# Norm sums held as rows, modulation columns 32 wide, and the first head's levels as two 64-wide blocks

## The reference

```python
sh1, sc1, gt1, sh2, sc2, gt2 = jnp.split(mod, 6, axis=-1)        # mod = silu(c) @ w_mod + b_mod
h = rmsnorm(x, lw['g_mix']) * (1.0 + sc1) + sh1
pq, pkv, pkr, hq, hf_f, hf_b, hi, hg, ga, gb = split_cols(h @ lw['w_in'])
q = (rmsnorm(pq, lw['g_q']) @ lw['w_uq'])                        # ...
ckv = rmsnorm(pkv, lw['g_kv'])                                    # ...
# four heads of a gated linear recurrence, forward and backward over the tokens:
o = rmsnorm(o_f + o_b, g_hg.reshape(HG_HEADS, HG_DV))
o = o.reshape(B, T, HG_WIDTH).astype(hq.dtype) * jax.nn.silu(hg)
```

## Time and profile before

| | us |
| --- | --- |
| median of 3 runs | 2058.93 |
| the runs' ends | 2056.06 to 2059.39 |
| the profiled execution's own time | 2058.16 |
| its span, first to last instruction | 2056.4 |
| busy: PE | 1994.0 |
| busy: DVE | 1120.0 |
| busy: ACT | 766.7 |
| busy: POOL | 831.9 |

### The profile page before, as it was taken

The page is one execution under the profiler, slowest core; times in us unless marked ns, Lnnn a source line. Parts: engine busy times, 40 slices in busy tenths (PEclk is TensorE's granted clock), DMA queues, the critical chain, the costliest instruction groups (busy, mean ns, idle before and its releaser), DMA issues.

```text
span 2056.4 us, 34056 instructions
## 1 busy us (share of the span) xinstructions
PE 1994.0 (97%) x13708; PEld 1837.9 (89%) x13708; DVE 1120.0 (54%) x1715; ACT 766.7 (37%) x1189; POOL 831.9 (40%) x595
## 2 busy tenths in 40 slices
PE   6999999999999989999999988999999999999998
PEld 5888999999999978887799877999999999988886
DVE  5314353526142047566535356988888888645363
ACT  4323233333223254767733234322222222353441
POOL 1225263535133235455535634433443443252441
PEclk9999999999999999999999999999999999999999
DMA  8563111112213284324266445422222231584661
GB/s 294 200 199 37 42 51 44 48 52 74 67 41 90 72 227 143 93 67 107 73 173 202 147 149 189 125 77 65 86 65 65 75 98 59 175 304 141 230 237 67
DMA packets 223310, 244.09 MB, mean 119 GB/s; under 512 B 57865, under 2 KB 184162, under 8 KB 223154
## 3 DMA queue, kind: packets, MB, share of 16 engines
q1 hardware_dynamic: 220962, 233.65, 37.3%
q0 software_dynamic: 2192, 8.26, 1.2%
HBM read 182.62 MB, written 59.26 MB: 118 GB/s over the span
## 4 chain that ended last, share of the span: by engine, by line
PE 53%; DVE 3%; DMA 3%; ACT 2%; POOL 1%; issue 1%; SPq 1%; DVEq 0%; ACTq 0%; POOLq 0%
PE late_psum L2938 22%; PE late_psum L2950 13%; PE late_psum L1876 4%; PE late_psum L1901 4%; PE late_psum L2897 3%; PE late_psum L2251 3%; PE late_psum L1511 1%; PE late_psum L1846 1%; DMA s_w_raw<-in_w_hg_o 1%; DVE p_lo L2056 1%; DMA scratch_extra<-e_lo 1%; DMA merge_gates<-scratch_gates 0%; DVE conv L3124 0%; ACT prob L1987 0%; PE late_psum L1515 0%
## 5 line engine op out<-in xcount | busy, mean ns | idle before, releaser
L688 PE MATMUL s_psum<-h_hi,s_w_hi 128*128 128x384 f32 x984 | 333.3, 344 | 6.4 <-DVE h_lo L1402 6.4
L688 PE MATMUL s_psum<-h_hi,s_w_lo 128*128 128x384 f32 x984 | 326.1, 337 | 0.0
L688 PE MATMUL s_psum<-h_lo,s_w_hi 128*128 128x384 f32 x984 | 325.9, 337 | 0.0
L131 POOL TENSOR_TENSOR s_w_lo<-s_w_raw,s_w_hi 128x1024 fp32r<-128x1024 f32 x41 | 100.0, 2440 | 337.0 <-ACT s_w_hi L126 337.0
L2938 PE MATMUL late_psum<-h_lo,ffn_w_hi 128*128 128x320 f32 (+1 forms) x704 | 208.5, 296 | 0.0
L2938 PE MATMUL late_psum<-h_hi,ffn_w_lo 128*128 128x320 f32 (+1 forms) x704 | 208.4, 296 | 0.0
L2938 PE MATMUL late_psum<-h_hi,ffn_w_hi 128*128 128x320 f32 (+1 forms) x704 | 208.3, 296 | 0.0
L688 PEld LDWEIGHTS s_psum<-h_hi,s_w_hi 128*128 128x128 f32 x984 | 185.5, 189 | 15.8 <-issue 14.0
L688 PEld LDWEIGHTS s_psum<-h_lo,s_w_hi 128*128 128x128 f32 x984 | 186.1, 190 | 0.0
L688 PEld LDWEIGHTS s_psum<-h_hi,s_w_lo 128*128 128x128 f32 x984 | 185.8, 189 | 0.0
L2873 POOL TENSOR_TENSOR u_lo<-u_raw,u_hi 128x384 fp32r<-128x384 f32 x66 | 112.9, 1719 | 162.5 <-ACT u_hi L2770 161.5
(11 more groups left out here) (371 smaller groups left out, 4709.9 us busy)
## 6 DMA issues: line engine op xcount, KB each, us to landing
w_raw<-in_w_ffn_out SPq DMA_DIRECT2D x66, 512.0 KB, 3.7
ffn_raw<-in_w_ffn_in SPq DMA_DIRECT2D x44, 512.0 KB, 5.3
s_w_raw<-in_w_in SPq DMA_DIRECT2D x41, 512.0 KB, 4.3
s_w_mod<-in_w_mod SPq DMA_DIRECT2D x8, 2048.0 KB, 8.3
scratch_u<-conv SPq DMA_DIRECT2D x22, 576.0 KB, 3.6
u_raw<-scratch_u SPq DMA_DIRECT2D x66, 192.0 KB, 5.2
scratch_gates<-sig SPq DMA_DIRECT2D x48, 192.0 KB, 1.9
merge_gates<-scratch_gates SPq DMA_DIRECT2D x16, 576.0 KB, 4.8
```

What stands on the lines that cost most here:

```text
L131: pool.tensor_tensor(flat[0], flat[1], flat[2], ALU.subtract).then_inc(self.lo_ready, 1)
L688: return pe.matmul(slot_bank(s), weights(c)[wx][:, k, :], hx[:, k, j * CH:(j + 1) * CH], start=(k == 0 and n == 0), stop=(k == KD - 1 and ...
```

## The change

- The norms' and heads' sums: three matmuls with 32 columns of ones as stationary (`ones[:, 0:BLOCK]`) and 384 tokens moving, chunk g into partitions 32g to 32g + 31 of one bank. The statistic is now 96x384 and lies in rows; root and reciprocal run on it, in place. The broadcast is three matmuls, one for each chunk, with a row of ones as stationary and the statistic's row moving.
- The columns of `m_rows` and `mod_rows` (`piece_columns`, `mod_columns`): 16 matmuls of 32x2 in place of 4 of 128x2, at 12 places.
- The first head's levels 1 to 6 (h == 0): two 64-wide blocks a tile in place of four of 32.
- The table: R, kv_rb, q_rb, q_apply, up_load and up_split one slot later. ACT's S waits for the R of the head before (`rb_ps`), since the statistic is in place. The heads' statistic lies on the memory of `mod_rows`.
- ACT's start: split(0) and split(1) move ahead of the last `x_take` and of `take_piece(0)`.

Lines number from the kernel before and after: after, the product is L692, the levels L829, S L898, R L906, the columns L781.

```diff
+ROWS = slice(0, NCH * BLOCK)
...
         self.acc = arena(f"{tag}_acc", [P, NT])
-        self.stat = arena(f"{tag}_stat", [P, 2 * TILES])
+        self.stat = arena(f"{tag}_stat", [P, CH])
...
         pe.wait_ge(self.acc_ready, self.kts - 1)
-        for t in range(TILES):
-            last = pe.matmul(psum[:, t:t + 1], self.acc[:, t * P:(t + 1) * P], self.cst.ones[:, 0:1], start=True, stop=True)
+        for g in range(NCH):
+            last = pe.matmul(psum[BLOCK * g:BLOCK * (g + 1), 0:CH], self.cst.ones[:, 0:BLOCK], self.acc[:, g * CH:(g + 1) * CH],
+                             start=True, stop=True)
...
         act.wait_ge(self.sums_ready, 1)
-        act.activation(self.stat[:, 0:TILES], psum[:, 0:TILES], ACT.Sqrt, scale=1.0 / self.width,
-                       bias=self.cst.eps[:, 0:1]).then_inc(self.std_ready, 1)
+        act.activation(self.stat[ROWS, :], psum[ROWS, 0:CH], ACT.Sqrt, scale=1.0 / self.width,
+                       bias=self.cst.eps[ROWS, 0:1]).then_inc(self.std_ready, 1)
...
         dve.wait_ge(self.std_ready, 1)
-        dve.reciprocal(self.stat[:, TILES:2 * TILES], self.stat[:, 0:TILES]).then_inc(self.rstd_ready, 1)
+        dve.reciprocal(self.stat[ROWS, :], self.stat[ROWS, :]).then_inc(self.rstd_ready, 1)
...
         pe.wait_ge(self.rstd_ready, 1)
-        for t in range(TILES):
-            last = pe.matmul(psum3[:, t // 3, (t % 3) * P:(t % 3 + 1) * P],
-                             self.stat[:, TILES + t:TILES + t + 1].to_broadcast([P, P]), self.cst.ident[:, :],
-                             start=True, stop=True)
+        for g in range(NCH):
+            row = slice(BLOCK * g, BLOCK * g + 1)
+            last = pe.matmul(psum3[:, g, 0:CH], self.cst.ones[row, :], self.stat[row, :], start=True, stop=True)
...
             at[a + 1 + lv].append(("L", h, lv))
-        for r, kind in ((9, "X"), (10, "U"), (12, "O"), (13, "S"), (14, "R")):
+        for r, kind in ((9, "X"), (10, "U"), (12, "O"), (13, "S"), (15, "R")):
...
             at[a - HG_PHASE + 15].append(("Q", h, 0))
-    for r, kind in ((6, "kv_square"), (7, "kv_sums"), (8, "kv_rb"), (9, "cache"), (10, "kv_apply"), (11, "key"),
-                    (13, "ckv_out"), (18, "q_square"), (20, "q_sums"), (21, "q_rb"), (22, "q_apply"), (26, "up_load"), (30, "up_split")):
+    for r, kind in ((6, "kv_square"), (7, "kv_sums"), (9, "kv_rb"), (9, "cache"), (10, "kv_apply"), (11, "key"),
+                    (13, "ckv_out"), (18, "q_square"), (20, "q_sums"), (22, "q_rb"), (23, "q_apply"), (27, "up_load"), (31, "up_split")):
...
         near = early("hg_near", [P, TILES, SIDE])
+        rows_at = early.at
...
         sel = early("mod_sel", [P, 8])
-        ostat = early("ostat", [P, 2 * TILES])
+        orow = Arena(nc, rows_at)("ostat", [P, CH])
...
                             a = 4 * x + 2 * j
-                            last = pe.matmul(psum[:, 7, a:a + 2], m_rows[i % 2][:, x, j * P:(j + 1) * P], sel[:, 0:2],
-                                             start=True, stop=True)
+                            for b in range(0, P, BLOCK):
+                                last = pe.matmul(psum[b:b + BLOCK, 7, a:a + 2], m_rows[i % 2][:, x, j * P + b:j * P + b + BLOCK],
+                                                 sel[:, 0:2], start=True, stop=True)
...
                         a = 8 * n + 2 * j
-                        last = pe.matmul(psum[:, 5, a:a + 2], mod_rows[n % 2][:, j * P:(j + 1) * P], sel[:, 0:2],
-                                         start=True, stop=True)
+                        for b in range(0, P, BLOCK):
+                            last = pe.matmul(psum[b:b + BLOCK, 5, a:a + 2], mod_rows[n % 2][:, j * P + b:j * P + b + BLOCK],
+                                             sel[:, 0:2], start=True, stop=True)
...
                                 t = 3 * g + x
+                                if h == 0 and 0 < lv < LEVELS:
+                                    b = 1 << (lv - 1)
+                                    for i in range(2):
+                                        dst = psum[i * SIDE:(i + 1) * SIDE, level_bank(n), x * SIDE:(x + 1) * SIDE]
+                                        own = t * P + i * SIDE
+                                        last = pe.matmul(dst.rearrange("p (n h b) -> p n h b", h=2, b=b),
+                                                         k_level[lv % 2][:, own:own + SIDE], sibling_view(qd, own, SIDE, b),
+                                                         start=True, stop=True)
+                                    continue
...
                         pe.wait_ge(osq_ready, 3 * h + 3)
-                        for t in range(TILES):
-                            last = pe.matmul(psum[:, S_BANK, t:t + 1], osq[:, t * P:(t + 1) * P], cst.ones[:, 0:1],
-                                             start=True, stop=True)
+                        for g in range(NCH):
+                            last = pe.matmul(psum[BLOCK * g:BLOCK * (g + 1), S_BANK, 0:CH], cst.ones[:, 0:BLOCK],
+                                             osq[:, g * CH:(g + 1) * CH], start=True, stop=True)
...
                         pe.wait_ge(gated_ready, 3 * h + 3)
-                        for t in range(TILES):
-                            last = pe.matmul(psum[:, rb_bank(t // 3), (t % 3) * P:(t % 3 + 1) * P],
-                                             ostat[:, TILES + t:TILES + t + 1].to_broadcast([P, P]), cst.ident[:, :],
-                                             start=True, stop=True)
+                        for g in range(NCH):
+                            row = slice(BLOCK * g, BLOCK * g + 1)
+                            last = pe.matmul(psum[:, rb_bank(g), 0:CH], cst.ones[row, :], orow[row, :], start=True, stop=True)
...
                         act.wait_ge(s_ps, h + 1)
-                        act.activation(ostat[:, 0:TILES], psum[:, S_BANK, 0:TILES], ACT.Sqrt, scale=1.0 / DK,
-                                       bias=cst.eps[:, 0:1]).then_inc(std_ready, 1)
+                        if h > 0:
+                            act.wait_ge(rb_ps, h)
+                        act.activation(orow[ROWS, :], psum[ROWS, S_BANK, 0:CH], ACT.Sqrt, scale=1.0 / DK,
+                                       bias=cst.eps[ROWS, 0:1]).then_inc(std_ready, 1)
...
                         x_take(2 * t - 3)
+                split(0)
+                split(1)
...
                 take_piece(0)
-                split(0)
-                split(1)
...
                         dve.wait_ge(std_ready, h + 1)
-                        dve.reciprocal(ostat[:, TILES:2 * TILES], ostat[:, 0:TILES]).then_inc(rstd_ready, 1)
+                        dve.reciprocal(orow[ROWS, :], orow[ROWS, :]).then_inc(rstd_ready, 1)
```

## The result

The changed kernel takes 2026.14 us (median of 4 runs, 2022.51 to 2027.25) against 2059.16 before (median of 4, 2056.06 to 2059.58): a ratio of 0.9843, 95% interval 0.9830 to 0.9857. That is 33 us off where 24.4 were forecast. The profiled execution of after is 2027.25 us long, against 2058.16: 30.9 off. It is the slowest of the four runs of after, 1.1 above their median.

The account below looks back on a forecast made before the run. TensorE, busy 97% of the span, was taken to bound the kernel; −3.8 − 2.5 − 6.0 − 6.2 − 6.2 + 2.3 − 3.0 + 1.0 = −24.4 against 2058.16 gave 2034 us, range 2025 to 2045.

Parts of the forecast that it names:

- start, POOL beside DVE: Before TensorE's first product: ACT's earlier splits let POOL's subtractions finish before DVE's gain_mix; −3.8 us.
- clock behind it: 8 us behind the start gap, clock at 0.50 of full: most of the lost work returns; −2.5 us.
- columns, 12 sites: Modulation columns: 32 records of 32x2 matmuls at 12 ns each replace a 0.88 us step; −6.0 us.
- S and R, 6 sites each: Norm sums and broadcast in four heads, kv, q: each 1.93 us falls to 0.9; −6.2 us apiece.
- levels 64 wide: First head's levels 1 to 6: 18 64-wide multiplications replace 36 32-wide, a loss of +2.3 us.
- stall: First head, 164.60 to 172.50: instructions late behind SP's `mod` stores; a third of 9.3 us goes, −3.0 us.
- q's new wait: Chunk after q_apply: POOL's qn_lo starts later, w_lo ends later, TensorE waits; +1.0 us.
- behind the first stage: After about 716 us: all that the change touches lies in the first stage, so no term was summed here.
- The rival in which a record needs 25 ns: Column steps: 32 records need 0.8 us, the 12 sites give only −1.0; 2038.8 us, chance 0.03.
- Row groups side by side: R's three one-row matmuls at partitions 0, 32, 64 overlap, 0.9 us; if in turn, 2.2, chance 0.22.
- the rival with stall and low clock gone: First head and start: stores no longer meet TensorE's packet, low clock vanishes; 6.3 and 1.5 more off, 2026, chance 0.13.
- The moved steps: R, kv broadcast, up_load and up_split one slot later: no cost; q_apply's move priced separately at +1.0 us.

Follow-up runs that it names:

- the kernel before with late stores: Kernel before the change, only SP's four row stores of `mod` moved from the first head's fourth slot to its thirteenth: 2047.93 us, ratio 0.9950.
- The kernel with 32-wide levels: Changed kernel with the first head's levels 1 to 6 as four 32-wide blocks again, nothing else: 2033.58 us, ratio 0.9884.
- the kernel with more instructions: Changed kernel with 32-wide levels in the first head and the last column step done three times over: 2034.16 us (2 runs), ratio 0.9883.

## Why the prediction was right, and where its sum was off

Step by step, in us, from starts of TensorE in the two profiled executions:

| step | forecast | shown |
| --- | --- | --- |
| start, POOL beside DVE | −3.8 | −3.7 (gap 6.45 to 2.76) |
| clock behind it | −2.5 | −2.4 (8 us at 0.80, not 0.50; varies) |
| columns, 12 sites | −6.0 | about −6 |
| S and R, 6 sites each | −12.4 | about −11.8 |
| levels 64 wide | +2.3 | +2.8 |
| stall | −3.0 | −9.1 |
| q's new wait | +1.0 | +1.0 (0.68 idle, the slots around it a little longer) |
| behind the first stage | 0 | −0.7 |

These add up to −29.9 of the 30.9; of the rest, 0.8 is that the first column step starts that much earlier in after (32.72 against 33.50). This varies without any edit of the start: the kernel before with late stores has it at 32.65. Against the forecast of −24.4, the difference of the two profiled executions is 6.5 larger, 6.1 of it the stall; the medians, 33.0 apart, add 2.1.

- **The start**: for the gap, mechanism and size hold, by the trace and by the run that undoes it. POOL's subtraction holds DVE up while both run. The clock's term is not fixed by the gap. The kernel with 32-wide levels has the same gap of 2.76 and no low clock behind it, by the same window as for after:

```profile
37.53:45.53 8.00, 7.85 (x108) 5.66 (x108) 4.11 (x9) 2.04 (x4) 0.00 (x0) 1.00 1.06 323
```

  So 1.6 us of the clock's term (0.20 of 8 us) come and go between executions with the same start, and its fit to −2.5 is in part luck.
- **Columns**: 32 records in 0.28 us, 8.8 ns each, even under the 12 that was taken. But the 24 products ahead of a 32-wide step take 0.1 more to the next start (before 4.27, after 4.36 to 4.37), so that the net is 0.5 a site, what was forecast. The rival in which a record needs 25 ns, drawn from the Trainium skill ("TensorE: Matmul & The Clock Gate", section "Wait — 56ns, not 53.3ns?"), falls: 32 of them would be 0.8, and the trace has 0.28.
- **S and R**: 0.78 and 0.85, forecast 0.9 each; the 0.1 given back by the products ahead brings it to the forecast value. Row groups side by side hold (0.85 against 2.12 in one group, 2.5 times). This agrees in kind with what the Trainium skill says of packing small matmuls (same page, section "Measured speedup vs the span model": 3.07 times for four row tiles); here it is three tiles.
- **Levels**: +2.76, forecast +2.3; the first two levels cost 1.66 and 1.28 rather than 1.20. Why they do isn't settled; it is so without the stores as well.
- **The stall**: this is the term that was mis-sized. The prediction read the place rightly, and by all that the runs show the mechanism, and took a third of it away for want of knowing where the packet would fall. It reasoned on the packet's position. That by itself made it worse: with all other edits in and the levels 32 wide, the stall costs 43.19 − 31.20 = 12.0 us, in before 40.87 − 31.46 = 9.4. What decides is how many instructions a level spends while a packet is late: 64-wide levels spend half. In both 32-wide kernels with the stores in place it is back, at two positions. Nearly the whole event went, 6.1 us more than was put in the sum, and this is most of the difference between 2034 and 2026. So the rival with stall and low clock gone came about for the stall, and for the start's clock in part (0.80), given 0.13; it should have had the larger chance, since "the level's packets are half" stood in the text and wasn't priced.
- **q's chain**: the wait came where it was put, with POOL's w_lo as its end, and 0.68 us long.
- **The later stages** are 0.7 shorter in this execution: the last product of the first stage starts 719.43 − 689.24 = 30.2 us earlier. Their gaps vary between executions by as much (the one ahead of the products of line 1511 is 2.0 us in before, 1.6 in after, and 2.0 in the kernel with more instructions), and no edit touches them.
- **The moved steps** cost nothing, and the reciprocal of 96x384 took 2.55 us where 2.7 was worked out from 128x1 and 128x9.

## What to carry to other kernels

A gap in the middle of an engine's row of like instructions, with no wait in it, points to an engine that lacks instructions, not data: look for what fills the queues then, and issue stores of single elements where TensorE spends few instructions. Of an edit that helps, ask whether it cures or covers: the wider blocks were worth some 8 us beside the stores and cost 2.8 without them. Where a large gap has a known cause, price what the change does to that cause as its own case, and don't take a fraction of it.

## What the runs showed of the hardware

- 32-wide matmuls with two columns go at 8.8 ns a record from start to start, 32 in 0.28 us; a step of them costs 0.1 us more on the row ahead.
- Three one-row matmuls (1x384, fp32) take 0.85 us in three row groups and 2.12 in one.
- DVE's work, even on a 128x4 tile, stretches from 0.16 to 2.00 us beside a running POOL subtraction; its four affine steps from 2.05 to 6.17.
- A reciprocal costs 2.55 us for 384 elements a partition, 6.6 ns each.
- Behind four stores of 1024 four-byte elements one packet of the instruction queue takes 4.5 to 7.3 us in place of 0.9 to 1.5, and TensorE stands without a wait, in gaps 8 to 19 us after the first store was issued. In a stretch of 3.16 us the transfer engines were busy 0.78 while moving 2 GB/s.
- Behind one and the same gap of 2.76 us the granted clock over 8 us was 0.80 in one kernel and 1.00 in another.
